# Latent attention scores from high and low parts: a two-block kernel on one core

## The chip, the cores and the metric

The kernel runs on one core of one Trainium2 chip. The core has the engines TensorE (PE), VectorE (DVE), ScalarE (ACT), GpSimd (POOL) and SyncE (SP, which issues most transfers), each with its own queue of instructions; semaphores order them. The metric is the device time of one execution in microseconds (us), median of several runs.

## The reference

Two blocks work on 512 tokens of 1024 features. The first block is untouched but for its last step, a norm, which is also the input norm of the second. What is computed in the second block (cut):

```python
h = _rms_norm(x, norm_g) * (1.0 + scale) + shift           # adaLN
dq, dk, dv, cq, ckv, kr, g = split(h @ w_in)
q_m = rms(cq) @ w_uq                                       # 4 heads x (128 nope + 64 rope)
k_nope = rms(ckv) @ w_uk ; v_m = rms(ckv) @ w_uv
q_m = _rms_norm(concat(q_nope, rope(q_pe)), mla_q_norm)
k_m = _rms_norm(concat(k_nope, rope(kr) for all heads), mla_k_norm)
logit_m = einsum('bqhd,bkhd->bhqk', q_m, k_m) * 192 ** -0.5        # latent heads
o_m = softmax(where(allowed, logit_m, -1e30)) @ v_m
logit_d = einsum('bqhcd,bkhcd->bchqk', dq, dk) * 64 ** -0.5 + bias  # 4 differential heads
attn_d = softmax(.)[:, 0] - lam * softmax(.)[:, 1]
o_d = _rms_norm(attn_d @ dv, diff_sub_norm) * (1 - lam_init)
out = x + gate * ((concat(o_d, o_m) * silu(g)) @ w_out)
```

## The kernel before

Data lie with features on the 128 rows and tokens along them (512 columns). Every projection is a product of three passes in the format fp32r: an operand is split into a high part (rounded) and a low part (the rest), and PE adds high by high, low by high and high by low (`mm3`, L962 to L964). The weights come in slabs; ACT copies the high part (`w_hi`, L582), DVE subtracts it for the low part (`weights_low`, L1610). Two slabs are in flight.

The final norm starts the second block: for each of eight feature tiles DVE computes hn (L1668), ACT copies h_hi (L650), POOL subtracts h_lo (L528), and PE opens its first projection tile. Behind the eight hn, DVE has the low part of the next weight slab, two step tiles of the bias and the reciprocal rsx, by which projections are scaled.

The projections that follow run in 34 numbered slots, one accumulation tile each; PE's `beside()` puts small matmuls between, and DVE's `evacuate()` empties the bank and does the slot's side work. Slots 26 to 33 are the eight tiles (128x256) of dv. In slots 28 to 33 the reciprocal norms of the latent heads are applied: PE's `widen` (L1034) spreads one row of `rs` over 128 rows of a bank, reading the 32 rows of `rs` of one quarter, and DVE's `scaled` (L1698) multiplies a tile of q (`qm`, tiles 0 to 3 nope, 4 and 5 the rope halves of two heads each), of k (`kn`) or of the rope part of k (`kp`) by it and by the gain. The list `WIDE` gives their order, two a slot.

The second attention consists of 32 units (`UNITS2`): v = 0 to 15 are latent, head v // 4 and query tile v % 4; v = 16 to 31 are differential. Each engine goes through them in a loop of its own:
- PE: `scores2(v + 2)`, `turn(v)` (four transposes of Pm, L1219), `values2(v - 1)` (L1516), and for v < 8 `widen_diff(v)` for dq and dk of the differential heads. A latent unit's scores are two fp32 matmuls: q nope by k nope (L1503) and the 64 rope rows (L1505).
- DVE: `weigh2(v)`, that is a reciprocal of the row sums (L1989) and the weighing of Pm (L2222; two operations, L2219 and L2220, in a differential unit), `peaks2(v + 2)` (mask or bias, and row maximum, L1974), for v < 8 `scaled` of dq or dk, and at v = 5, 9, 13 and so on `head_out`, a copy of a head's output out of its bank (L2226).
- ACT: `exps(v + 1)` (L747) and `evac(v)`, the copy of the turned Pm to PTm (L757). Scores of unit v + 2 wait for exp of unit v, whose bank they take.
- POOL adds the mask to the bias tiles of the differential heads (L533), which SP loads.

Then come the gate zg and the output projection.

## Time and profile before

| | us |
|---|---|
| median of three runs | 1823.74 (1819.90 to 1824.51) |
| the profiled execution | 1826.18 |
| its span | 1824.4 |
| PE busy | 1765.4 (97%) |
| DVE busy | 1030.8 (57%) |
| ACT busy | 627.8 (34%) |
| POOL busy | 86.0 (5%) |
| mean granted clock of PE | 0.990 |

An engine's busy time is the sum of its instructions in one profiled execution; the span runs from the first to the last. A chain of waits follows the end of the program back, from each piece of work to what released it. The granted clock is a share of 2.4 GHz. The final norm lies at 1441 to 1462 of the span, the second attention at 1604 to 1722.

### The profile page before, as it was taken

How to read it: one execution, taken by the hardware profiler on the slowest of the kernel's cores; microseconds unless marked ns; L12 is line 12 of the kernel's file. 1: busy time of each engine (PE TensorE's matmuls, PEld its weight loads, DVE VectorE, ACT ScalarE, POOL GpSimd, SP SyncE). 2: the span in 40 equal slices, each digit the busy share in tenths (PEclk: the TensorE clock that was granted, in tenths of full speed). 3: DMA queues.
4: the chain of work that ended last, by engine and by line, in shares of the span. 5: the costliest groups of instructions: out<-in, count | busy, mean ns of one | idle time of the engine just before them, and what ended most of it. 6: DMA issues, size and time to landing. Idle time of an engine off the chain costs nothing.

```text
span 1824.4 us, 22833 instructions
## 1 busy us (share of the span) xinstructions
PE 1765.4 (97%) x9171; PEld 1362.3 (75%) x9171; DVE 1030.8 (57%) x1645; ACT 627.8 (34%) x1047; POOL 86.0 (5%) x92
## 2 busy tenths in 40 slices
PE   7999999999988889999999999999999999999899
PEld 6888888887765557877888888888888666645677
DVE  5665444456566655437544457633544677756764
ACT  4221222231246761323322243312223566324631
POOL 0000000000012320000000000000000200011100
PEclk9999999899989999999999999999999999999999
DMA  6545332252200003212333233233332332201212
GB/s 215 182 165 187 113 108 76 64 186 94 70 1 1 2 1 115 82 58 70 93 101 106 93 99 92 86 94 110 94 100 80 89 101 94 86 23 36 73 59 89
DMA packets 232428, 163.60 MB, mean 90 GB/s; under 512 B 9372, under 2 KB 220548, under 8 KB 232196
## 3 DMA queue, kind: packets, MB, share of 16 engines
q1 hardware_dynamic: 230004, 157.95, 28.3%
q10 hardware_dynamic: 2320, 4.20, 0.6%
q8 instruction: 73, 1.20, 0.3%
q14 instruction: 31, 0.25, 0.0%
HBM read 155.84 MB, written 6.29 MB: 89 GB/s over the span
## 4 chain that ended last, share of the span: by engine, by line
PE 91%; DVE 6%; POOL 2%; issue 1%; SPq 0%; ACT 0%; DMA 0%; DVEq 0%
PE bank L962 24%; PE bank L964 24%; PE bank L963 24%; PE bank L1219 3%; PE bank L1207 2%; DVE bank L1974 2%; PE bank L1243 2%; PE bank L1386 1%; PE bank L1034 1%; PE bank L1041 1%; PE bank L1300 1%; PE bank L1516 1%; POOL Pm L521 1%; PE bank L1505 1%; PE bank L1174 1%
## 5 line engine op out<-in xcount | busy, mean ns | idle before, releaser
L962 PE MATMUL bank<-h_hi,w_hi 128*128 128x512 f32 x1200 | 478.9, 399 | 5.5 <-POOL h_lo L528 4.0
L964 PE MATMUL bank<-h_hi,w_lo 128*128 128x512 f32 x1200 | 467.5, 390 | 0.0
L963 PE MATMUL bank<-h_lo,w_hi 128*128 128x512 f32 x1200 | 467.5, 390 | 0.0
L582 ACT ACTIVATE w_hi<-w_raw 128x2048 fp32r<-128x2048 f32 (+3 forms) x134 | 236.8, 1767 | 525.2 <-PE bank L964 525.2
L1610 DVE TENSOR_TENSOR w_lo<-w_raw,w_hi 128x2048 fp32r<-128x2048 f32 (+3 forms) x134 | 283.4, 2115 | 56.9 <-ACT w_hi L582 54.5
L962 PEld LDWEIGHTS bank<-h_hi,w_hi 128*128 128x128 f32 x1200 | 225.3, 188 | 70.0 <-issue 17.7
L963 PEld LDWEIGHTS bank<-h_lo,w_hi 128*128 128x128 f32 x1200 | 225.3, 188 | 49.4 <-issue 4.1
L964 PEld LDWEIGHTS bank<-h_hi,w_lo 128*128 128x128 f32 x1200 | 225.2, 188 | 47.5
L962 PE MATMUL bank<-u_hi,w_hi 128*128 128x512 f32 x352 | 138.0, 392 | 0.0
L963 PE MATMUL bank<-u_lo,w_hi 128*128 128x512 f32 x352 | 137.9, 392 | 0.0
L964 PE MATMUL bank<-u_hi,w_lo 128*128 128x512 f32 x352 | 137.7, 391 | 0.0
L1616 DVE TENSOR_TENSOR act_f<-bank,rsx 128x512 f32<-128x512 f32 x44 | 30.4, 690 | 165.2 <-PE bank L964 165.2
L1219 PEld LDWEIGHTS bank<-cst,Pm 128*128 128x128 f32 x448 | 48.5, 143 | 89.3 <-POOL Pm L521 47.3
L747 ACT ACTIVATE Pm<-bank,mstat 128x512 f32<-128x512 f32 (+3 forms) x176 | 99.1, 572 | 34.8 <-DVE mstat L1974 33.3
L757 ACT ACTIVATE PTm<-bank 128x512 f32<-128x512 f32 (+3 forms) x160 | 68.1, 467 | 118.0 <-PE bank L1219 117.8
L1219 PE MATMUL bank<-cst,Pm 128*128 128x128 f32 x448 | 71.4, 289 | 33.3 <-POOL Pm L521 22.1
L697 ACT ACTIVATE silu<-silu 128x512 f32<-128x512 f32 x44 | 27.8, 632 | 199.2 <-DVE silu L1616 199.2
L1974 DVE CUSTOM_DVE_ANT_0 bank<-bank,mask 128x128 f32<-128x128 f32 (+3 forms) x128 | 60.5, 515 | 58.0 <-PE bank L1207 57.6
L521 POOL TENSOR_SCALAR Pm<-Pm,mstat,gates 128x128 f32<-128x128 f32 (+3 forms) x64 | 49.8, 779 | 628.6 <-DVE mstat L1989 628.6
L963 PEld LDWEIGHTS bank<-u_lo,w_hi 128*128 128x128 f32 x352 | 66.6, 189 | 14.0
L964 PEld LDWEIGHTS bank<-u_hi,w_lo 128*128 128x128 f32 x352 | 66.6, 189 | 13.9
L962 PEld LDWEIGHTS bank<-u_hi,w_hi 128*128 128x128 f32 x352 | 66.7, 189 | 13.9
(400 smaller groups left out, 2421.0 us busy)
## 6 DMA issues: line engine op xcount, KB each, us to landing
w_raw<-in_w_in SPq DMA_DIRECT2D x28, 1024.0 KB, 5.2
w_raw<-in_ffn_w_gate SPq DMA_DIRECT2D x44, 512.0 KB, 3.6
w_raw<-in_ffn_w_up SPq DMA_DIRECT2D x44, 512.0 KB, 4.8
w_raw<-in_ffn_w_down SPq DMA_DIRECT2D x32, 704.0 KB, 4.4
ada_w<-in_ada_w SPq DMA_DIRECT2D x16, 768.0 KB, 6.0
w_raw<-in_w_in SPq DMA_DIRECT2D x19, 512.0 KB, 4.0
w_raw<-in_w_out SPq DMA_DIRECT2D x8, 1024.0 KB, 5.0
w_raw<-in_w_branch_nsa SPq DMA_DIRECT2D x8, 512.0 KB, 5.1
```

Of the source, the lines that this page charges most:

```text
L521: pool.tensor_scalar(p_, p_, mstat[:, u % 2, 6:7], gates[:, t, g0:g0 + 1], ALU.mult, ALU.mult).then_inc(sem("p_ready"), 1)
L582: act.activation(w_hi[s % 2][:, 0:n], w_raw[s % 2][:, 0:n], ACT.Copy).then_inc(s_hi, 1)
L747: last = act.activation(Pm[u % 2][:, i, 0:n], bank[2 * (u % 2) + i][:, 0:n], ACT.Exp, bias=mstat[:, u % 2, 2 + i:3 + i], scale=scale, accu ...
L757: last = act.activation(PTm[u % 2][:, i, 0:n], bank[4 + i][:, 0:n], ACT.Copy)
L962: pe.matmul(o, l[0], r[0], start=first, stop=False)
L963: pe.matmul(o, l[0], r[1], start=False, stop=False)
L964: return pe.matmul(o, l[1], r[0], start=False, stop=last)
L1207: ins = pe.matmul(bank[2 * (u % 2) + e][:, 0:n], qT[r, hp, t * P:(t + 1) * P], kz[r, br, g, 0:n], start=True, stop=True)
L1219: ins = pe.transpose(bank[4 + i][:, b * P:(b + 1) * P], Pm[u % 2][:, i, b * P:(b + 1) * P], ident)
L1243: ins = pe.matmul(place(e, t), vtok[:, b, c:c + 64], PTm[u % 2][:, e, b * P:(b + 1) * P], start=u in FIRST and b == 0, stop=False)
L1610: dve.tensor_sub(w_lo[s % 2][:, 0:n], w_raw[s % 2][:, 0:n], w_hi[s % 2][:, 0:n]).then_inc(s_lo, 1)
L1974: return dve.tensor_tensor_reduce(s_, s_, add, -scale, 3.0e38, ALU.add, ALU.min, mstat[:, u % 2, 2 + i:3 + i])
```

## The change

1. Final norm: h_lo is subtracted by DVE (`low3`), one tile behind hn, instead of by POOL. The last square of the token norm is added by PE (a second matmul) and not by DVE.
2. dv tiles are evacuated by ACT with a scale for each row instead of by DVE.
3. `WIDE` has ten entries instead of twelve, in slots 28 to 32. The rope part of k is one tile for each head (`kp[h]`), both halves of its rows filled, a further DVE product by the bank that k uses.
4. `high_parts` on ACT copies four high parts for each head (q, k, rope of q on its own 64 rows, kp): heads 0 and 1 in slots 31 and 33, heads 2 and 3 behind `evac` of units 0 and 2. `low_part` on DVE subtracts the low parts: heads 0 and 1 in the same slots, heads 2 and 3 one part a unit, v = 0 to 7. The low half of rope q goes to the other 64 rows of `q_rope[h]`.
5. `weights_low` of the slab behind (zg's first) moves from slot 29 to slot 33.
6. A latent unit's scores are five fp32r matmuls: q_hi k_hi, q_hi k_lo, q_lo k_hi, and the stacked rope parts of 128 rows by kp_hi and by kp_lo.
7. Latent units are weighed by ACT (a Copy scaled by the reciprocal), between `exps(v + 1)` and `evac(v)`, instead of by DVE.
8. `widen_diff` and its `scaled` move from v = 0..7 to v = 8..15; the load of the first bias tiles waits for the scores of unit 7.

```diff
+        WH, WL = -32 + 8 * spare, -16 + 8 * spare
+        part = lambda name, kb, dt=F32R: at(name, [P, S], dt, ARENA + kb * KB)[:, :]
+        q_hi = [part(f"q_hi{h}", kb) for h, kb in enumerate((24, 40, WH, WL))]
+        k_hi = [part(f"k_hi{h}", kb) for h, kb in enumerate((26, 42, WH + 2, WL + 2))]
+        q_rope = [part(f"q_rope{h}", kb) for h, kb in enumerate((28, 44, WH + 4, WL + 4))]
+        kp_hi = [part(f"kp_hi{h}", kb) for h, kb in enumerate((30, 56, WH + 6, WL + 6))]
+        KP_AT = (48, 50, 58, 94)
+        kp = [part(f"kp{h}", kb, F32) for h, kb in enumerate(KP_AT)]
+        kp_lo = [part(f"kp_lo{h}", kb) for h, kb in enumerate(KP_AT)]
+        q_lo = at("q_lo", [P, 4, S], F32R, ARENA + 60 * KB)
+        k_lo = at("k_lo", [P, 4, S], F32R, ARENA + 72 * KB)
...
-                                sp.wait_ge(sem("wide_used"), 15)
+                                sp.wait_ge(sem("s_full"), U0 + 8)
...
-            for k in range(KD):
-                pool.wait_ge(sem("h_hi_ready"), 3 * KD + k + 1)
-                pool.tensor_sub(h_lo[:, k, :], hn[k % 4][:, :], h_hi[:, k, :]).then_inc(sem("h_ready"), 1)
...
-        WIDE = [("q", 0), ("k", 0), ("qp", 0), ("kp", 0), ("q", 1), ("k", 1), ("q", 2), ("k", 2), ("qp", 1), ("kp", 1), ("q", 3), ("k", 3)]
-        HEAD_WIDE = (7, 9, 13, 15)
+        WIDE = [("q", 0), ("k", 0), ("qp", 0), ("q", 1), ("k", 1), ("q", 2), ("k", 2), ("qp", 1), ("q", 3), ("k", 3)]
...
+            def high_parts(h):
+                e, done_wide = h % 2, (5, 8, 10, 13)[h]
+                own = slice(64 * e, 64 * e + 64)
+                act.wait_ge(sem("wide_used"), max(done_wide, 6 if h == 0 else 11 if h == 2 else 0))
+                act.activation(q_hi[h], qm[:, h, :], ACT.Copy).then_inc(sem("head_hi"), 1)
+                act.activation(k_hi[h], kn[:, h, :], ACT.Copy).then_inc(sem("head_hi"), 1)
+                act.activation(q_rope[h][own, :], qm[own, 4 + h // 2, :], ACT.Copy).then_inc(sem("head_hi"), 1)
+                act.activation(kp_hi[h], kp[h], ACT.Copy).then_inc(sem("head_hi"), 1)
...
+                act.wait_ge(acc_full, a + 1)
+                act.wait_ge(acc_free, a)
+                s, t = i // 4, i % 4
+                act.activation(dv[:, t, s * 256:(s + 1) * 256], bank[a % 4][:, 0:256], ACT.Copy, scale=col[:, G_RST + t:G_RST + t + 1]).then_inc(acc_free, 1)
+                if i == 4:
+                    for b in range(2):
+                        act.wait_ge(sem(f"bias_stored{b}"), 128)
+                if i in (5, 7):
+                    high_parts(i // 2 - 2)
...
             for v in range(len(UNITS2)):
...
+                if v < 16:
+                    act.wait_ge(sem("sum_ready"), attended(U0 + v))
+                    p0 = Pm[(U0 + v) % 2][:, 0, :]
+                    act.activation(p0, p0, ACT.Copy, scale=mstat[:, (U0 + v) % 2, 6:7]).then_inc(sem("pm_ready"), 1)
                 evac(U0 + v, S, 1)
+                if v in (0, 2):
+                    act.wait_ge(acc_full, first_acc["zg"])
+                    high_parts(2 + v // 2)
...
                 if n == 3:
-                    pe.wait_ge(sem("sqg_added"), 7)
-                    pe.matmul(bank[4][:, :], ones, sqgsum[:, :], start=True, stop=True).then_inc(sem("gmm"), 1)
+                    pe.wait_ge(sem("sqg_added"), 6)
+                    pe.matmul(bank[4][:, :], ones, sqgsum[:, :], start=True, stop=False)
+                    pe.wait_ge(sem("nsqg"), KD)
...
+                if U0 <= u < U0 + 16:
+                    pe.wait_ge(sem("pm_ready"), u - U0 + 1)
+                else:
+                    pe.wait_ge(sem("p_ready"), attended(u) if u < U0 else attended(u) - 16)
...
-                if 28 <= slot < 34:
+                if 28 <= slot < 33:
                     for what, i in WIDE[2 * slot - 56:2 * slot - 54]:
-                        if what in ("q", "k"):
+                        if what == "qp":
+                            widen(2, i, 4, 2)
+                        else:
                             widen(2, (0, 2)[what == "k"] + i // 2, 4 + i % 2)
-                        else:
...
-                if t == 0:
-                    pe.wait_ge(sem("wide_used"), HEAD_WIDE[h] if kind else 17 + 2 * h)
+                if t == 0 and kind:
+                    pe.wait_ge(sem("head_split"), 4 * h + 4)
+                elif t == 0:
+                    pe.wait_ge(sem("wide_used"), 15 + 2 * h)
...
-                    pe.matmul(bank[b][:, :], qm[:, h, q], kn[:, h, :], start=True, stop=False)
-                    r = slice(64 * (h % 2), 64 * (h % 2) + 64)
-                    ins = pe.matmul(bank[b][:, :], qm[r, 4 + h // 2, q], kp[r, h // 2, :], start=False, stop=True)
+                    pe.matmul(bank[b][:, :], q_hi[h][:, q], k_hi[h], start=True, stop=False)
+                    pe.matmul(bank[b][:, :], q_hi[h][:, q], k_lo[:, h, :], start=False, stop=False)
+                    pe.matmul(bank[b][:, :], q_lo[:, h, q], k_hi[h], start=False, stop=False)
+                    pe.matmul(bank[b][:, :], q_rope[h][:, q], kp_hi[h], start=False, stop=False)
+                    ins = pe.matmul(bank[b][:, :], q_rope[h][:, q], kp_lo[h], start=False, stop=True)
...
-                if v < 8:
-                    widen_diff(v)
+                if 8 <= v < 16:
+                    widen_diff(v - 8)
...
-                if n == 3:
+                if n == 3 and k < KD - 1:
...
+                def low3(k):
+                    dve.wait_ge(sem("h_hi_ready"), 3 * KD + k + 1)
+                    tick(dve.tensor_sub(h_lo[:, k, :], hn[k % 4][:, :], h_hi[:, k, :]), "h_ready")
                 dve.wait_ge(sem("token_std"), 1)
                 for k in range(KD):
                     if k >= 4:
                         dve.wait_ge(sem("h_ready"), 3 * KD + k - 3)
                     dve.wait_ge(sem("xg_ready"), k + 1)
                     tick(dve.scalar_tensor_tensor(hn[k % 4][:, :], std[:, :], col[:, G_MOD + k:G_MOD + k + 1], xg[:, k, :], ALU.mult, ALU.add), "hn_ready")
+                    if k:
+                        low3(k - 1)
+                low3(KD - 1)
...
+            def spread(what, i):
+                if what == "k":
+                    j = count.get("wide_used", 0)
+                    dve.wait_ge(sem("wide_full"), j + 1)
+                    done(dve.scalar_tensor_tensor(kp[i], ckr[:, 1, :], col[:, G_KP:G_KP + 1], wide_bank(j)[:, :], ALU.mult, ALU.mult))
+                    scaled(kn[:, i, :], kn[:, i, :], G_KN)
+                elif what == "q":
+                    scaled(qm[:, i, :], qm[:, i, :], G_QN)
+                else:
+                    scaled(qm[:, 4 + i, :], qm[:, 4 + i, :], G_QP)
+            def low_part(h, i):
+                own, other = (slice(64 * e, 64 * e + 64) for e in (h % 2, 1 - h % 2))
+                dve.wait_ge(sem("head_hi"), 4 * h + i + 1)
+                if i == 0:
+                    ins = dve.tensor_sub(q_lo[:, h, :], qm[:, h, :], q_hi[h])
+                elif i == 1:
+                    ins = dve.tensor_sub(k_lo[:, h, :], kn[:, h, :], k_hi[h])
+                elif i == 2:
+                    ins = dve.tensor_sub(q_rope[h][other, :], qm[own, 4 + h // 2, :], q_rope[h][own, :])
+                else:
+                    ins = dve.tensor_sub(kp_lo[h], kp[h], kp_hi[h])
+                tick(ins, "head_split")
...
-                    scale_rows(dst, t, 256)
+                    acc_at[0] += 1
...
-                if slot >= 28:
-                    for j in (2 * slot - 56, 2 * slot - 55):
-                        scaled(*spread[j])
+                if 28 <= slot < 33:
+                    for what, i in WIDE[2 * slot - 56:2 * slot - 54]:
+                        spread(what, i)
+                if slot in (31, 33):
+                    for i in range(4):
+                        low_part((slot - 31) // 2, i)
...
-                if slot in (1, 3, 5, 7, 9, 15, 17, 25, 29):
+                if slot in (1, 3, 5, 7, 9, 15, 17, 25, 33):
...
+                if kind:
+                    return
...
-                else:
-                    tick(dve.tensor_scalar(p0, p0, st[:, 6:7], None, ALU.mult), "p_ready")
...
                 if v < 8:
-                    d = (dq, dk)[v % 2][:, v // 2, :]
+                    low_part(2 + v // 4, v % 4)
+                elif v < 16:
+                    d = (dq, dk)[v % 2][:, v // 2 - 4, :]
                     scaled(d, d, (G_DQ, G_DK)[v % 2])
                 if v >= 5 and v % 4 == 1:
```

DVE from the end of the dv slots to the first reciprocal of the attention (L1974 and L2024 are the peaks; each has a second row that reads its result). Before:

```order
L1619 TENSOR_SCALAR dv<-bank,col 128x256
L1698 SCALAR_TENSOR_TENSOR qm<-qm,col,bank 128x512
L1698 SCALAR_TENSOR_TENSOR kn<-kn,col,bank 128x512
L1974 ISA bank,mstat<-bank,cst 128x512
L1974 ISA mstat 128x1
L1974 ISA bank,mstat<-bank,hidden_215 128x512
```

After:

```order
L1748 SCALAR_TENSOR_TENSOR kn<-kn,col,bank 128x512
L2194 TENSOR_TENSOR q_lo<-qm,q_hi_227 128x512
L2196 TENSOR_TENSOR k_lo<-kn,k_hi_231 128x512
L2198 TENSOR_TENSOR q_rope_235<-qm,q_rope_235 64x512
L2200 TENSOR_TENSOR kp_lo_247<-kp_243,kp_hi_239 128x512
L1654 TENSOR_TENSOR w_lo_60<-w_raw_56,w_hi_58 128x2048
L2024 ISA bank,mstat<-bank,cst 128x512
L2024 ISA mstat 128x1
L2024 ISA bank,mstat<-bank,hidden_214 128x512
```

Four low parts of head 1 and the low part of zg's first slab now stand ahead of the first peaks; the evacuation of dv (L1619) is gone.

DVE in the loop of the attention, at v = 4 and 5 before and v = 8 and 9 after, where the second of the two has a `head_out` (L2226, now L2302). Before:

```order
L1698 SCALAR_TENSOR_TENSOR dq<-dq,col,bank 128x512
L1989 RECIPROCAL mstat<-mstat 128x1
L2222 TENSOR_SCALAR Pm_123<-Pm_123,mstat 128x512
L1974 ISA bank,mstat<-bank,cst 128x512
L1974 ISA mstat 128x1
L1698 SCALAR_TENSOR_TENSOR dk<-dk,col,bank 128x512
L2226 COPY cst<-bank 128x512
L1989 RECIPROCAL mstat<-mstat 128x1
L2222 TENSOR_SCALAR Pm_122<-Pm_122,mstat 128x512
```

After:

```order
L1748 SCALAR_TENSOR_TENSOR dq<-dq,col,bank 128x512
L2039 RECIPROCAL mstat<-mstat 128x1
L2024 ISA bank,mstat<-bank,cst 128x512
L2024 ISA mstat 128x1
L1748 SCALAR_TENSOR_TENSOR dk<-dk,col,bank 128x512
L2302 COPY cst<-bank 128x512
L2039 RECIPROCAL mstat<-mstat 128x1
L2024 ISA bank,mstat<-bank,cst 128x512
L2024 ISA mstat 128x1
```

The weighing (L2222) no longer follows the reciprocal; the scaled products (now L1748) stand ahead of the reciprocal as before, in the later units.

ACT from the first exp on (L747, now L755; L757, now L765). Before:

```order
L747 ACT_TABLE_LOAD
L747 ACTIVATE Pm_122,mstat<-bank,mstat 128x512
L747 ACTIVATE Pm_123,mstat<-bank,mstat 128x512
L757 ACTIVATE PTm_124<-bank 128x512
L747 ACTIVATE Pm_122,mstat<-bank,mstat 128x512
L757 ACTIVATE PTm_125<-bank 128x512
```

After:

```order
L755 ACTIVATE Pm_122,mstat<-bank,mstat 128x512
L755 ACTIVATE Pm_123,mstat<-bank,mstat 128x512
L952 ACTIVATE Pm_122<-Pm_122,mstat 128x512
L765 ACTIVATE PTm_124<-bank 128x512
L919 ACTIVATE q_hi_228<-qm 128x512
L920 ACTIVATE k_hi_232<-kn 128x512
L921 ACTIVATE q_rope_236<-qm 64x512
L922 ACTIVATE kp_hi_240<-kp_244 128x512
L755 ACTIVATE Pm_122,mstat<-bank,mstat 128x512
L952 ACTIVATE Pm_123<-Pm_123,mstat 128x512
```

The weighing (L952) stands between exp and the copy of the turned unit, and the four Copies of head 2 (L919 to L922) stand behind the copy of unit 0 and ahead of exp of unit 2.

## Rows read from the trace of the kernel before

**Rows 1.** windows; columns: stretch, us, busy PE PEld DVE ACT POOL, clock, DMA

```profile
1612.00:1648.00 36.00, 35.76 (x157) 16.96 (x158) 18.94 (x43) 9.91 (x25) 1.77 (x2) 1.00 0.00 0
1648.00:1667.00 19.00, 19.00 (x94) 10.54 (x93) 8.45 (x25) 7.09 (x18) 0.00 (x0) 1.00 0.00 1
```

**Rows 2.** timeline of the final norm: start, length, engine, work, idle before

```profile
1446.07 1.41 DVE L1668 SCALAR_TENSOR_TENSOR tmp<-std,col,xg 128x512 f32<-128x512 f32 x2 [1.79 <-ACT std L643]
...
1451.44 1.79 DVE L1668 SCALAR_TENSOR_TENSOR tmp<-std,col,xg 128x512 f32<-128x512 f32 x1
...
1461.12 0.50 PE L962 MATMUL bank<-h_hi,w_hi 128*128 128x512 f32 x1 [1.62 <-POOL h_lo L528]
```

**Rows 3.** chain of waits: start, length, what; final norm, then one matmul

```profile
1447.56 13.51 POOL h_lo L528 x7
...
1461.62 0.23 PE bank L963
```

**Rows 4.** ScalarE (ACT) and VectorE work by form, whole span: count, busy, mean ns

```profile
L614 ACT ACTIVATE h_hi<-x,col 128x512 fp32r<-128x512 f32 x20 | 14.3, 713 | 36.8 <-DVE x L2117 24.1 <-DVE x L1613 7.6 <-DVE x L1852 5.1
...
L650 ACT ACTIVATE h_hi<-tmp 128x512 fp32r<-128x512 f32 x4 | 2.5, 626 | 0.9 <-DVE tmp L1668 0.9
...
L1610 DVE TENSOR_TENSOR w_lo<-w_raw,w_hi 128x2048 fp32r<-128x2048 f32 x98 | 225.6, 2303 | 44.3 <-ACT w_hi L582 42.4
...
L1637 DVE TENSOR_TENSOR sqsum<-sqsum,sq 128x512 f32<-128x512 f32 x12 | 8.3, 688 | 0.2
```

**Rows 5.** chain of waits, slots before the second attention

```profile
1562.08 1.84 PE bank L1018 x8
...
1598.91 1.02 PE bank L1034 x8
```

**Rows 6.** timeline, first turn of the second attention

```profile
1610.30 0.66 PE L1219 MATMUL bank<-cst,Pm 128*128 128x128 f32 x4
```

**Rows 7.** chain of waits, a latent unit with a widening

```profile
1643.47 1.00 PE bank L1034 x4
1644.47 1.06 PE bank L1503 x2
1645.53 1.05 PE bank L1505 x2
...
1647.16 0.89 PE bank L1516 x8
```

**Rows 8.** chain of waits, a unit with head_out

```profile
1635.08 0.76 DVE dk L1698
...
1635.86 0.70 DVE cst L2226
...
1636.58 0.17 DVE mstat L1989
```

**Rows 9.** chain of waits around the end of the second attention

```profile
1715.58 0.56 DVE Pm L2219
...
1716.16 0.76 DVE Pm L2220
```

**Rows 10.** windows of granted clock, after idle PE; columns as in rows 1

```profile
494.00:499.00 5.00, 1.00 (x6) 0.50 (x6) 4.58 (x19) 1.92 (x9) 0.51 (x1) 1.00 0.00 0
499.00:506.00 7.00, 5.84 (x22) 2.61 (x20) 5.25 (x23) 2.71 (x12) 1.42 (x3) 0.50 0.02 5
506.00:512.50 6.50, 6.50 (x29) 4.58 (x30) 1.46 (x7) 2.10 (x8) 0.48 (x1) 0.50 0.00 0
...
1716.00:1717.00 1.00, 0.03 (x1) 0.03 (x1) 0.96 (x3) 0.28 (x2) 0.00 (x0) 1.00 0.00 0
...
1718.00:1721.00 3.00, 3.00 (x17) 3.00 (x16) 0.36 (x1) 0.86 (x2) 0.00 (x0) 0.51 0.00 0
1721.00:1724.00 3.00, 3.00 (x21) 2.69 (x20) 0.69 (x1) 0.85 (x2) 0.00 (x0) 1.00 0.02 5
```

**Rows 11.** timeline, PE's first wait for the final norm

```profile
1449.41 0.47 PE L962 MATMUL bank<-h_hi,w_hi 128*128 128x512 f32 x1 [2.42 <-POOL h_lo L528]
```

More of the change, by code:

```diff
@@ L406, in build @@
         N_VEC_DMAS = len(VECS) - 1 + 2 * len(HALF_VECS)
+        pair_units = lambda hp, ts: [(hp, t, br) for t in ts for br in range(2)]
+        second = pair_units(1, (3, 2, 1, 0))
+        UNITS = pair_units(0, range(NT))
+        for t in range(NT):
+            UNITS += [(None, t, None), second[t]]
+        COMPRESSED = len(UNITS) - 2
+        UNITS += second[4:]
+        for hp in range(2, 8):
+            UNITS += pair_units(hp, range(NT))
+        U0 = len(UNITS)
+        FIRST = [min(u for u in range(U0) if UNITS[u][0] == hp) for hp in range(8)]
+        FULL_AT = {COMPRESSED: 0}
+        for hp in range(1, 8):
+            FULL_AT[max(u for u in range(U0) if UNITS[u][0] == hp)] = hp
+        attended = lambda u: u + 1 - sum(1 for w in UNITS[:u + 1] if w[0] is None)
         @block.sync
@@ L493, in _ @@
             sp.wait_ge(sem("out_stored"), 32 * NT)
-        pair_units = lambda hp, ts: [(hp, t, br) for t in ts for br in range(2)]
-        second = pair_units(1, (3, 2, 1, 0))
-        UNITS = pair_units(0, range(NT))
-        for t in range(NT):
-            UNITS += [(None, t, None), second[t]]
-        COMPRESSED = len(UNITS) - 2
-        UNITS += second[4:]
-        for hp in range(2, 8):
-            UNITS += pair_units(hp, range(NT))
-        U0 = len(UNITS)
-        FIRST = [min(u for u in range(U0) if UNITS[u][0] == hp) for hp in range(8)]
-        FULL_AT = {COMPRESSED: 0}
-        for hp in range(1, 8):
-            FULL_AT[max(u for u in range(U0) if UNITS[u][0] == hp)] = hp
-        attended = lambda u: u + 1 - sum(1 for w in UNITS[:u + 1] if w[0] is None)
         @block.gpsimd
@@ L915, in _ @@
             each_slab("ukv", rest_squares, 8)
-            each_slab("dv", all_norms, 4)
+            each_slab("dv", diff_values, 4)
             exps(U0, 0, S, 1, -1.0)
@@ L1005, in big_norm @@
                 if n == 3:
-                    pe.wait_ge(sem("sqg_added"), 7)
-                    pe.matmul(bank[4][:, :], ones, sqgsum[:, :], start=True, stop=True).then_inc(sem("gmm"), 1)
+                    pe.wait_ge(sem("sqg_added"), 6)
+                    pe.matmul(bank[4][:, :], ones, sqgsum[:, :], start=True, stop=False)
+                    pe.wait_ge(sem("nsqg"), KD)
+                    pe.matmul(bank[4][:, :], ones, sqg[(KD - 1) % 2][:, :], start=False, stop=True).then_inc(sem("gmm"), 1)
                 pe.wait_ge(sem("sq_added"), 7 * n)
@@ L1440, in beside @@
                     pe.wait_ge(sem("bias_out"), 16)
-                if 28 <= slot < 34:
+                if 28 <= slot < 33:
                     for what, i in WIDE[2 * slot - 56:2 * slot - 54]:
-                        if what in ("q", "k"):
+                        if what == "qp":
+                            widen(2, i, 4, 2)
+                        else:
                             widen(2, (0, 2)[what == "k"] + i // 2, 4 + i % 2)
-                        else:
-                            widen(2, (0, 2)[what == "kp"] + i, 4, 2)
             def widen_diff(j):
@@ L2127, in _ @@
             STEPS_BEHIND = {1: 2, 2: 1, 3: 2, 4: 1, 5: 2, 6: 2, 7: 1, 8: 2, 16: 2}
-            spread = [(qm[:, i, :], qm[:, i, :], G_QN) if what == "q" else (kn[:, i, :], kn[:, i, :], G_KN) if what == "k"
-                      else (qm[:, 4 + i, :], qm[:, 4 + i, :], G_QP) if what == "qp" else (kp[:, i, :], ckr[:, 1, :], G_KP) for what, i in WIDE]
+            def spread(what, i):
[20 more added lines that the diff above has]
+                tick(ins, "head_split")
             def evacuate(dst, t=None):
@@ L2142, in evacuate @@
                     copy_tile(dst)
-                freed()
+                if t is None:
+                    freed()
                 if slot == 3:
@@ L2161, in evacuate @@
                     dve.wait_ge(sem("rst_full"), 2)
-                    done(dve.tensor_copy(col[:, G_RST:G_RST + NT], bank[4][:, 0:NT]))
+                    done(dve.tensor_copy(col[:, G_RST:G_RST + NT], bank[4][:, 0:NT]), "rst_ready")
                 if slot == 26:
```

12 lines of the change are left out of this document (6 added, 6 removed).

## Prediction

> **What bounds the kernel now.** Read the table of the profile first: TensorE (PE) is busy for 97% of the span, so an edit pays only where PE waits or where PE's own work gets shorter. Then the windows of the second attention: from 1612 to 1648, where each unit also carries a widening, PE is busy 35.76 of 36.00 us, and from 1648 to 1667, latent units alone, 19.00 of 19.00, while VectorE (DVE) is busy for about half of either and ScalarE (ACT) for under 0.4 [rows 1]. PE is the bound there. The chain of waits gives one such unit piece by piece: widening 1.00, scores 1.06 and 1.05, transposes 0.59, values 0.89, in all 4.59 [rows 7]. Outside the attention, the place to see is the final norm: the chain passes through GpSimd (POOL) for 13.51 us, PE starts only after 2.42 idle and stands idle 1.62 before the last of the eight tiles [rows 2, 3, 11].
>
> **Final norm: −2.0.** The eight h_lo subtractions leave POOL, where seven take 13.51 [rows 3], for DVE. DVE's own steps there cost 0.70 each when POOL is silent (1.41 for two) and up to 1.79 beside it [rows 2]; a 128x512 subtraction or sum of two SBUF tiles is 0.69 [rows 4]. Sixteen at 0.70 from 1446.07, with 0.4 for the first wait on ACT, end at 1457.7, where POOL ended at 1461.07. Next on DVE is the low part of the following weights, 2.30 [rows 4], so it is ready at about 1460.2 and PE opens its second projection tile there. Before, that tile began six matmuls of 0.23 [rows 3] after 1461.12, at 1462.5. That is −2.3; I take −2.0 for the hops between engines. Bounds: the idle of 1.62 goes at least, less 0.4 of hops (−1.2); at most DVE keeps nothing of its queue in PE's way and the 3.4 less 0.3 come through (−3.1). That PE adds the last square itself (one fp32 matmul more) I take at nothing: ACT's table load stands behind that spot and covers it; uncovered, about 0.5.
>
> **The dv slots: +0.9.** The pairs of widenings stand in five slots instead of six, −1.0 (1.02 for eight matmuls, one pair [rows 5]). But the pair (q-rope 0, q 1) now reads the same 32 rows of rs twice. The nearest rows: eight small matmuls of alternating row groups take 1.02, and eight where groups repeat take 1.84 [rows 5]; so +0.8. PE then waits for ACT, which now evacuates dv behind its Copies, which take 0.63 each [rows 4]: a wait of about half a Copy in each of three slots and one hop, +1.1. Bounds 0 (no wait, the pair overlaps) to +1.9. The four extra DVE products for the rope part of k (0.75 each) lie in slots where PE works for 4 us and DVE for about 2: nothing, and as much as 0.75 for the last of them.
>
> **Start of the attention: +2.0.** Before, the last dv matmul is followed 7.4 us later by the first turn, at 1610.30 [rows 6]. After (in before's time), from 1602.9: dv evacuation 0.4, then ACT's four high parts of head 1, each 0.63 long [rows 4] and about 0.52 apart, and DVE's four low parts of 0.69 behind them, until 1606.9; then w_lo of zg's first slab, 2.30, which now stands straight ahead of the first peaks (the first piece of order), until 1609.2; peaks 0.7, exp 0.69, peaks of unit 1, exp, and ACT's weighing 0.71 [rows 4], so that the first turn is at 1612.3. Bounds: +0.5 (w_lo alone, partly under the scores) and +3.5 (Copies at their full length and no overlap).
>
> **Units 0 to 7: −9.1.** Before, from the turn at 1610.30 to the end of the scores at 1646.58: 36.2 for eight units [rows 6, 7]. After, the widening is gone and the latent scores are five single-pass matmuls of 0.23 [rows 3] with 0.1 for the switch of type: 1.25 instead of 2.11. PE's unit is 0.66 + 0.89 + 1.25 = 2.8. Six units at 2.85 are 17.1. In units 0 and 2, ACT has four Copies more, behind its evacuation and ahead of the next exp (the third piece of order): 0.5 + 4 x 0.52 + 0.69 + 0.71 + turn 0.66 = 4.65, twice 9.3. With 0.4 for head_out at unit 5 and 0.3 of hops, 27.1. Bounds: 22.8 (ACT hidden) and 31 (weighing on ACT holds every unit up by 0.5).
>
> **Units 8 to 15: +9.6.** The widenings land here, and with cheap scores there is nothing left to hide DVE's answer. DVE's order is peaks, scaled dq or dk, head_out, reciprocal (the second piece of order); the reciprocal of the next unit stands behind scaled, which waits for the widening, which PE runs after turn and values. So each step is turn 0.66, values 0.89, widening 1.00, scaled 0.76, reciprocal 0.17 [rows 6 to 8], ACT's weighing 0.71 [rows 4], with hops 4.33. Seven steps are 30.3, and head_out [rows 8] at units 9 and 13 adds 1.4: 31.7. Before, they took 22.0, all of it PE's work [rows 1]: five steps of 3.39 (4.59 less the widening and the 0.2 by which the scores' first matmul is longer behind one) and two of 2.54, whose scores are those of a differential unit (1.06). The last step, to unit 16, waits in the same way and has the two DVE operations of a differential unit, 0.56 and 0.76 [rows 9]: +0.9, at most +1.9. What the change gains in the first half is given back in the second: the total of the widenings is the same, the saved scores (16 x 0.86 = 13.8) turn into waits for DVE and ACT.
>
> Sum so far: −2.0 + 0.9 + 2.0 − 9.1 + 9.6 + 0.9 = +2.3. The later stages are the same; POOL's bias sums, which stood in units 0 to 3, stand at units 7 to 9 and finish long before unit 16 asks for them.
>
> **The clock: +2.1.** In my walk PE has no work between the scores of unit 1 (about 1605.8) and those of unit 2 (about 1610.6), which wait for exp: over 4.5 us idle, just before the attention. What rows show: with PE busy 1.00 of 5 us its granted clock was 0.50 for the 13.5 us from 499 to 512.5; after some 2 us idle (0.03 busy from 1716 to 1717) it was 0.51 for 3 us and back at 1.00 from 1721 [rows 10]; after 2.42 idle at 1449.41 it stayed at 1.00 [rows 11]. So a fall to 1.2 GHz is likely. At half clock a unit of 2.8 takes 5.6; a dip like the shorter one (some 4.2 us) costs half its length, 2.1.
>
> The Trainium skill ("TensorE: Matmul & The Clock Gate", section "Why this matters for your kernels") speaks against the change here: an idle gap between bursts of matmuls sends the clock back to half. By that rule the sum is +4.4, and by the row at 1449.41, where a gap was forgiven, it is +2.3.
>
> Total +4.4. The profiled execution of before took 1826.18 (span 1824.4), so after's would be 1830.6; the median of before is 1823.74, and the forecast for the median is 1828.1, no change within 0.3% (5.5 us, about what a measurement of this kernel can tell).
>
> **Rivals.**
> - *The clock holds* (0.18): +2.3, 1826.0. For it stands the row at 1449.41; against it the length of this gap.
> - *Slower: the low clock lasts as long as at 499* (0.22). Price: for 13.5 us at 1.2 GHz, PE-bound units of 5.6 against 3.6 on average, so 2.4 units done where 3.7 would be: 4.8 us lost. 2.3 + 4.8 = +7.1, 1830.8. It decides against the forecast once the dip lasts over about 6 us. For it: units 0 and 2 leave PE idle for 2 of their 4.65 us, as thin a load as from 499 to 506.
> - *Slower: ACT is the bound of the first half too* (0.10): exp, weighing, evacuation and the wait between them hold each unit up by 0.5; 8 x 0.5 = 4 more on top of the forecast, +8.4, 1832.1. Rows for it: none of before has ACT between the reciprocal and the turn; against it, ACT's busy time of 1.9 in a unit of 2.8.
> - *Faster: the second half is bound by PE* (0.10). If the reciprocal came before scaled, a unit would be 0.66 + 0.89 + 1.00 + 1.15 = 3.7: 8 x 0.63 + 1.4 = 6.4 less, with the final norm at its better end 1.1 less: 2.3 − 7.5 = −5.2, and −6.0 if the row groups overlap as well: 1817.7. The clock must hold too. The order of DVE speaks against it.
> - *It doesn't do what it says*: the five passes are not 0.23 apart, since each switches between tiles of another row count. 0.2 more for each unit in the PE-bound half, +1.6: +6.0, 1829.7 (0.06). For it, the first scores matmul is 1.06 behind a widening of 32 rows [rows 7], longer than elsewhere; against it, every fp32r triple stands 0.23 apart.
>
> **How the numbers follow.** The forecast has a chance of 0.34. Faster by over 0.3%: 0.10. Slower: 0.22 + 0.10 + 0.06 = 0.38. Within: 0.34 + 0.18 = 0.52. The range goes from the faster rival, 1817.5, to 1835: the rival with ACT (+8.4) and the upper ends of the norm (0.8), the dv slots (1.0) and the last step (1.0), +11.2.
>
> **What would show it.** In the profile after: the last h_lo near 1457.7 and no POOL work from 1440 to 1470; an idle PE of over 4 us just before the first turn and a clock of 0.5 behind it; units 0 to 7 about 27 us long, with two of 4.6; units 8 to 15 at 4.3 with PE waiting for ACT's Pm, and 5.0 at the two with head_out. It would be wrong if units 8 to 15 run at 3.7, if the first units are as slow as the last, or if the clock never falls.

## The result

| | before | changed |
|---|---|---|
| median, 11 runs each | 1822.79 us (1817.98 to 1825.25) | 1829.15 us (1825.87 to 1834.14) |
| ratio to before | | 1.0036, 95% interval 1.0025 to 1.0047 |
| span of the profiled execution | 1824.4 us | 1826.9 us |
| mean granted clock | 0.990 | 0.988 |

The change costs 6.6 us (4.6 to 8.6), by the ratio. The forecast was 1828.1, +4.4; the time lies in its range. The forecast gave a slowing of over 0.3% a chance of 0.38 and a time within 0.3% one of 0.52; 0.36% is just on the slow side of that line, and the interval holds both sides. Of all executions of the kernels in this document one, of the kernel with latent units weighed by DVE, took 9859.93 us; its ratio leaves it out, and nothing here explains it.

The windows of the changed kernel, by the same columns as [rows 1]:

```profile
1440.00:1480.00 40.00, 38.48 (x230) 24.64 (x232) 35.05 (x45) 26.88 (x39) 0.00 (x0) 1.00 0.26 85
...
1604.00:1612.00 8.00, 5.36 (x20) 4.25 (x19) 2.89 (x8) 4.77 (x12) 0.00 (x0) 0.71 0.00 0
1612.00:1648.00 36.00, 31.70 (x178) 23.89 (x177) 16.16 (x38) 20.89 (x44) 5.90 (x4) 0.93 0.09 30
1648.00:1667.00 19.00, 15.44 (x85) 8.61 (x84) 8.64 (x22) 9.32 (x19) 1.26 (x1) 1.00 0.04 14
```

PE, which had 35.76 of 36 us and 19.00 of 19 in before [rows 1], has 31.70 and 15.44: PE no longer bounds these units by itself, and its clock falls in them. ACT's busy time in the first of the two stretches has doubled (20.89 for 9.91).

**By stage.** From the start of one piece of work to the start of the next, in the timelines of both traces, from the final norm's table load (1443.87 before, 1439.08 after; the 4.8 us ahead of it are told below):

| stretch | before | changed | difference | forecast |
|---|---|---|---|---|
| table load to the first step matmuls | 23.00 | 18.49 | −4.5 | −2.0 |
| to the first scores of the attention | 137.10 | 138.91 | +1.8 | +2.9 |
| first scores to turn 0 | 6.33 | 9.20 | +2.9 | (in the line above) |
| turn 0 to turn 8 | 36.21 | 29.29 | −6.9 | −9.1 |
| turn 8 to turn 15 | 22.04 | 31.94 | +9.9 | +9.6 |
| turn 15 to turn 16 | 4.14 | 5.84 | +1.7 | +0.9 |
| turn 16 to turn 31 | 46.43 | 49.27 | +2.8 | 0 |
| turn 31 to the end | 105.28 | 104.88 | −0.4 | 0 |
| the clock, by itself | | | (within the lines) | +2.1 |

The second block takes 7.3 us longer. The spans differ by 2.5 only, for in this pair of executions the changed kernel came to the table load 4.8 us earlier, in code that is the same.

### The profile page after: what moved, and what is told of

It is laid out like the page before. It is cut to its first block, busy times and chain, and to the rows that moved or that the text cites. A ratio compares the mean times of both kernels' runs of the same rounds, so it can differ in the third digit from the quotient of the medians.

```text
span 1826.9 us, 22889 instructions
## 1 busy us (share of the span) xinstructions
PE 1756.9 (96%) x9181; PEld 1370.0 (75%) x9181; DVE 1027.3 (56%) x1646; ACT 650.2 (36%) x1087; POOL 71.1 (4%) x84
## 4 chain that ended last, share of the span: by engine, by line
PE 90%; DVE 6%; issue 1%; ACT 1%; POOL 1%; SPq 0%; DMA 0%; DVEq 0%; ACTq 0%
PE bank L997 25%; PE bank L998 24%; PE bank L999 24%; PE bank L1259 3%; PE bank L1244 2%; PE bank L1283 2%; DVE bank L2024 2%; PE bank L1071 1%; PE bank L1426 1%; PE bank L1078 1%; PE bank L1340 1%; PE bank L1560 1%; POOL Pm L533 1%; PE bank L1211 1%; DVE Pm L2297 1%
## 5 line engine op out<-in xcount | busy, mean ns | idle before, releaser
L755 ACT ACTIVATE Pm<-bank,mstat 128x512 f32<-128x512 f32 (+3 forms) x176 | 99.0, 572 | 17.7 <-DVE mstat L2024 16.4
L765 ACT ACTIVATE PTm<-bank 128x512 f32<-128x512 f32 (+3 forms) x160 | 68.1, 467 | 99.7 <-PE bank L1259 99.5
L2024 DVE CUSTOM_DVE_ANT_0 bank<-bank,mask 128x128 f32<-128x128 f32 (+3 forms) x128 | 60.5, 514 | 56.9 <-PE bank L1244 56.5
L1902 DVE SCALAR_TENSOR_TENSOR x<-bank,x 128x512 f32<-128x512 f32 x32 | 22.1, 691 | 95.2 <-PE bank L999 95.2
```

The lines of the kernel that those rows point to most:

```text
L755: last = act.activation(Pm[u % 2][:, i, 0:n], bank[2 * (u % 2) + i][:, 0:n], ACT.Exp, bias=mstat[:, u % 2, 2 + i:3 + i], scale=scale, accu ...
L765: last = act.activation(PTm[u % 2][:, i, 0:n], bank[4 + i][:, 0:n], ACT.Copy)
L2024: return dve.tensor_tensor_reduce(s_, s_, add, -scale, 3.0e38, ALU.add, ALU.min, mstat[:, u % 2, 2 + i:3 + i])
```

## What the traces show

**Final norm.** Timeline of before (the last two of POOL's eight subtractions), then of the changed kernel:

```profile
1457.75 4.74 POOL L528 TENSOR_TENSOR h_lo<-sqg,h_hi 128x512 fp32r<-128x512 f32 x2
```

```profile
1443.56 0.47 PE L997 MATMUL bank<-h_hi,w_hi 128*128 128x512 f32 x1 [1.52 <-DVE h_lo L1709]
...
1452.28 2.29 DVE L1654 TENSOR_TENSOR w_lo<-w_raw,w_hi 128x2048 fp32r<-128x2048 f32 x1
...
1454.67 0.45 PE L997 MATMUL bank<-h_hi,w_hi 128*128 128x512 f32 x1
```

POOL's last pair ends at 1462.49. The 13.51 of [rows 3] are seven of eight subtractions, and 1461.07 is the end of the seventh; the forecast took it for the end of all. In the changed kernel DVE keeps ahead of PE, which needs 1.37 for the six matmuls of each h_lo and shows no wait after its start at 1443.56. The low part of the weights ends at 1454.57 and PE opens the next tile at 1454.67, when the 48 matmuls ahead of it are done: it holds nothing up.

**Start of the attention and its clock.** Timeline and windows of the changed kernel:

```profile
1603.52 0.65 PE L1545 MATMUL bank<-k_hi,q_hi 128*128 128x512 f32 x1 [4.48 <-ACT Pm L755]
...
1610.78 1.12 PE L1259 MATMUL bank<-cst,Pm 128*128 128x128 f32 x4 [2.64 <-ACT Pm L952]
```

```profile
1599.10:1603.50 4.40, 0.00 (x0) 0.00 (x0) 4.21 (x6) 1.79 (x4) 0.00 (x0) 1.00 0.00 0
1603.80:1607.10 3.30, 3.30 (x11) 2.61 (x11) 0.76 (x2) 1.27 (x4) 0.00 (x0) 0.50 0.00 0
1608.20:1610.80 2.60, 0.03 (x1) 0.03 (x1) 1.85 (x6) 2.52 (x6) 0.00 (x0) 0.95 0.00 0
1610.80:1613.60 2.80, 2.80 (x13) 2.80 (x14) 0.00 (x0) 1.67 (x4) 0.00 (x0) 0.50 0.00 0
1617.50:1619.70 2.20, 0.00 (x0) 0.00 (x0) 1.47 (x4) 2.15 (x5) 0.00 (x0) 1.00 0.00 0
1620.80:1624.10 3.30, 3.30 (x13) 2.71 (x12) 0.30 (x1) 1.50 (x4) 0.00 (x0) 0.50 0.02 5
1670.60:1672.70 2.10, 0.00 (x0) 0.00 (x0) 2.06 (x3) 0.00 (x0) 1.03 (x1) 0.83 0.00 0
1672.70:1678.40 5.70, 5.65 (x20) 3.92 (x21) 3.28 (x10) 1.94 (x5) 1.27 (x1) 0.50 0.15 46
```

Four idle stretches of PE (0.00 to 0.03 busy, the first number behind the length), and each is followed by matmuls at half clock: 4.4 us idle before the scores of unit 2, about 2.6 and 2.2 in units 0 and 2 while ACT makes the high parts of heads 2 and 3, and 2.1 before turn 16. The forecast had one dip, of 4.2 us. There are four, three of about 3 us and one of about 6. A fifth, from 1719.6 to 1723.2, has its like in before, behind 1717 [rows 10].

**Units 8 to 15.** The chain of waits of the changed kernel, a unit without head_out and the head of one with it:

```profile
1636.51 1.03 PE bank L1071 x4
...
1637.57 0.76 DVE dq L1748
...
1638.35 0.18 DVE mstat L2039
...
1638.55 0.73 ACT Pm L952
...
1639.32 0.66 PE bank L1259 x4
1639.98 0.89 PE bank L1560 x8
...
1641.92 0.76 DVE dk L1748
...
1642.71 0.70 DVE cst L2302
```

It is the forecast's chain link for link (widening, scaled, reciprocal, weighing, turn, values): 4.36 us from turn to turn, and 5.08 where head_out stands in it. [Rows 7] had PE's own work in this place.

## The experiments

All medians and ratios are of several runs beside the kernel before on the same chip; the changed kernel stands at 1.0036.

### The final norm by itself

The kernel before, with DVE's subtractions alone (the last square stays with DVE):

```diff
             for k in range(KD):
-                pool.wait_ge(sem("h_hi_ready"), 3 * KD + k + 1)
-                pool.tensor_sub(h_lo[:, k, :], hn[k % 4][:, :], h_hi[:, k, :]).then_inc(sem("h_ready"), 1)
...
+                    if k:
+                        low3(k - 1)
+                low3(KD - 1)
```

> The kernel before with one part of the change: the eight h_lo subtractions of the final norm by DVE, alternating with hn; all else as before. Theory from the two traces: PE reached the first step matmuls of the second projection tile 23.07 us after the norm's table load in before and 18.56 after it in after, so this part alone gives about -4.5 us (ratio 0.9975). Rival, the forecast's own term: -2.0 (0.9989), with the low part of the weights (2.3) ahead of PE's second tile. Second rival: nothing, since the eight subtractions only move the wait to the evacuation.

1816.35 us, ratio 0.9974 (0.9959 to 0.9988): −4.7 us. The first step matmuls come 18.50 behind the table load, in the changed kernel 18.49: the square that PE adds costs nothing, for from the step matmuls ahead of it to the table load both take 2.71. So the rest of the change costs 1.0036 − 0.9974, about 11 us.

### The reciprocal ahead of the scaled product

```diff
+            early = lambda v: 9 <= v < 17
             for v in range(len(UNITS2)):
-                weigh2(v)
+                if not early(v):
+                    weigh2(v)
                 if v + 2 < len(UNITS2):
                     peaks2(v + 2)
+                if early(v + 1):
+                    weigh2(v + 1)
```

> The changed kernel with one difference: for units 9 to 16 DVE does the reciprocal of the row sums (and unit 16's two weighing operations) ahead of the scaled dq or dk of the unit before, not behind it. Theory: in units 8 to 15 the chain widening, scaled, reciprocal, ACT's weighing, turn is what ends last (4.36 us a unit, 5.08 with head_out); taken out of it, PE's own work of 3.7 to 3.8 us a unit remains, and the stretch from turn 8 to turn 16 (37.8 us) falls to about 30.5 to 31.5: -6 to -7 us against the changed kernel, about level with before (ratio 1.000). Rival: ACT's queue (exp, weighing, copy) is the bound there, and the stretch falls by under 2.

1820.40 us, 0.9986 (0.9972 to 0.9999): −9 us against the changed kernel. Its chain of waits in this stretch is PE alone:

```profile
1642.13 1.00 PE bank L1071 x4
1643.14 0.43 PE bank L1545
1643.56 0.23 PE bank L1546
1643.79 0.24 PE bank L1547
1644.03 0.23 PE bank L1548
1644.26 0.24 PE bank L1549
1644.50 0.44 PE bank L1259 x4
1644.94 0.89 PE bank L1560 x8
```

That is 3.69 a unit. Turn 8 to 15 took 26.13 for 31.94, turn 15 to 16 3.54 for 5.84: −8.1, more than the 6 to 7 expected. With the idle stretch ahead of turn 16 the dip behind it went too (3.11 from turn 16 to 17 for 4.77). ACT's queue is not the bound here. This was the forecast's rival on the fast side, which it set aside because the order of DVE speaks against it: rightly for the kernel as it was, and the cure is that order.

### PE kept busy where it was idle

```diff
             scores2(1)
+            for _ in range(5):
+                pe.matmul(bank[1][:, :], ident[:, :], hidden[3], start=True, stop=True)
...
+                if v in (1, 3):
+                    for _ in range(2):
+                        pe.matmul(bank[1][:, :], ident[:, :], hidden[3], start=True, stop=True)
                 turn(U0 + v, NT, 1)
```

> The changed kernel with fp32 matmuls of 128x512 that nothing reads added on PE, where it is idle: five ahead of the scores of unit 2 (4.48 us idle), two ahead of the turns of units 1 and 3 (2.64 and 2.26 idle). Theory: idle PE is what takes the clock to half; kept busy it stays at 1.00, the three dips near 1604, 1611 and 1621 (3.2 us each) go, and the stretch from the first scores of unit 2 to turn 4 is 2 to 3.5 us shorter: -2 to -3.5 against the changed kernel. Rival: the dips are not tied to the idle stretches, the clock falls as often, and the time is the same or up to 1 us more for fillers that stick out.

1824.48 us, 1.0009 (0.9995 to 1.0024): −4.9 us with added work that nobody needs. Windows of this kernel over the first units:

```profile
1606.00:1612.00 6.00, 5.82 (x21) 3.05 (x20) 4.33 (x8) 2.64 (x7) 0.00 (x0) 1.00 0.00 0
1612.00:1620.00 8.00, 6.84 (x39) 4.88 (x38) 3.73 (x10) 6.51 (x15) 0.00 (x0) 1.00 0.00 0
1620.00:1630.00 10.00, 9.46 (x55) 7.02 (x55) 4.29 (x12) 7.71 (x17) 0.00 (x0) 1.00 0.05 6
```

All at 1.00. First scores to turn 0 took 8.32 (9.20 in the changed kernel), turn 0 to 8 26.21 (29.29): 4.0 us of the two stretches were the three dips. That is nearly half of what PE had stood idle in these places (9.4), on top of it. Later in the attention, where nothing was filled, the same trace shows two idle stretches:

```profile
1663.00:1664.70 1.70, 0.23 (x2) 0.00 (x1) 1.66 (x5) 0.72 (x1) 0.00 (x0) 1.00 0.00 0
1664.70:1668.20 3.50, 3.50 (x14) 2.67 (x16) 0.55 (x2) 1.93 (x5) 0.34 (x1) 0.53 0.20 75
1674.30:1676.50 2.20, 0.00 (x0) 0.00 (x0) 2.17 (x3) 0.00 (x0) 1.46 (x1) 1.00 0.00 0
1676.50:1680.00 3.50, 3.38 (x23) 2.43 (x24) 3.31 (x10) 2.12 (x6) 0.00 (x0) 1.00 0.28 75
```

Behind the shorter one, 1.47 ahead of turn 15, the clock fell (+1.6, a dip that the changed kernel doesn't have), and behind the longer one, 2.2 ahead of turn 16, it held: turn 16 to 17 took 2.70, where the changed kernel with the same wait took 4.77. So filling the idle stretches removed the dips behind them, but an idle stretch does not by its length decide whether a dip follows. The Trainium skill ("TensorE: Matmul & The Clock Gate", section "Why this matters for your kernels") warns of idle gaps between bursts; this run agrees with it, as the dips behind the three that were filled are gone. It warns of longer gaps than the 2.64 and 2.26 that had a dip behind them here; there the measurement decides.

### The weights' low part back in slot 29

```diff
-                if slot in (1, 3, 5, 7, 9, 15, 17, 25, 33):
+                if slot in (1, 3, 5, 7, 9, 15, 17, 25, 29):
```

> The changed kernel with the low part of zg's first weight slab (DVE, 2.3 us) back in slot 29, as before the change, instead of ahead of the first peaks. Theory: it stands on the path to the first exp, so the first turn comes 2.2 us earlier, PE's idle stretch shrinks from 4.5 to 2.3 us, and the clock may hold there: -2.2 to -3.5 against the changed kernel. Rival: slot 29 has no room on DVE and the 2.3 reappear as a PE wait for the widening banks in slots 30 and 31: no gain.

1827.19 us, 1.0018 (1.0004 to 1.0033): about −3.3, in an interval that overlaps that of the changed kernel; the trace shows where it comes from. First scores to turn 0: 6.12 for 9.20, that is 2.2 of DVE work and 0.9 of a dip that is gone. Turn 0 to 8 took 27.65 for 29.29, with one dip less. The slots took the same time (138.87 from the step matmuls to the first scores, 138.91 in the changed kernel), so slot 29 had room.

### Widenings of like width paired

```diff
-        WIDE = [("q", 0), ("k", 0), ("qp", 0), ("q", 1), ("k", 1), ("q", 2), ("k", 2), ("qp", 1), ("q", 3), ("k", 3)]
+        WIDE = [("q", 0), ("k", 0), ("qp", 0), ("qp", 1), ("q", 1), ("k", 1), ("q", 2), ("k", 2), ("q", 3), ("k", 3)]
...
-                e, done_wide = h % 2, (5, 8, 10, 13)[h]
+                e, done_wide = h % 2, (5, 9, 11, 13)[h]
```

> The changed kernel with another order of the ten widenings: both rope halves of q (two matmuls of 64 columns each) stand as one pair, instead of one beside q of head 1 and one beside k of head 2. Theory: in the changed kernel both mixed pairs take 2.05 us on PE where pairs of like width take 1.02 to 1.06, although the second mixed pair reads two different groups of 32 rows; what runs one after the other is the different width of the output, so all five pairs at about 1.05 give -2.0 against the changed kernel. Rival, the forecast's reason (the same 32 rows read twice, in the first mixed pair alone): -1.0.

1827.64 us, 1.0028 (1.0015 to 1.0041): −1.5, an interval that by itself leaves the size open; the chain of waits does not. A mixed pair of the changed kernel:

```profile
1586.69 2.05 PE bank L1071 x6
```

and two rows of this one, pairs of two halves each and of two whole widths:

```profile
1583.77 1.02 PE bank L1071 x8
1587.84 1.06 PE bank L1071 x4
```

From the step matmuls to the first scores it took 136.86 for 138.91, −2.05. The mixed pair shown is k of head 2 (rows 96 to 127 of rs) and q-rope of heads 2 and 3 (rows 32 to 63): different rows, and still one after the other. The forecast's reason, the same 32 rows read twice, would have spared this pair. That the width of the output is what matters fits all rows seen here; whether it is the columns or the change of form between two matmuls was not separated.

### High parts one a unit

```diff
-                if v in (0, 2):
+                if v < 8:
                     act.wait_ge(acc_full, first_acc["zg"])
-                    high_parts(2 + v // 2)
+                    high_parts(2 + v // 4, (v % 4,))
```

The low parts of heads 2 and 3 follow one unit later, v = 1 to 8.

> The changed kernel with the eight high parts of heads 2 and 3 on ACT one a unit (units 0 to 7) instead of four behind unit 0 and four behind unit 2, and the low parts one unit later. Theory: units 0 and 2 (5.10 and 4.91 us, PE idle 2.64 and 2.26 in them) fall to about 3, and two of the three clock dips go with the idle stretches: turn 0 to turn 8 from 29.3 to 24 to 25.5, -4 to -5 against the changed kernel. Rival: one Copy of 0.5 a unit on ACT makes all eight units ACT-bound at 3.4 and the stretch is 27 or more.

1826.82 us, 1.0014 (1.0001 to 1.0026): −4. Turn 0 to 8 took 25.79 for 29.29, but not as the theory had it in full: six of the eight units take 3.14 where PE needs 2.5. The long units are gone and one dip of the three is left. Later a dip ahead of turn 15 is new (+1.6) and the one behind turn 16 is missing (−2.1), as with the fillers. Each unit has the chain of turn, ACT's copy of it, one high part, exp and weighing, as the rival said, at a lower price than it said.

### Latent units weighed by DVE

```diff
-                if v < 16:
-                    act.wait_ge(sem("sum_ready"), attended(U0 + v))
-                    p0 = Pm[(U0 + v) % 2][:, 0, :]
-                    act.activation(p0, p0, ACT.Copy, scale=mstat[:, (U0 + v) % 2, 6:7]).then_inc(sem("pm_ready"), 1)
...
+                else:
+                    tick(dve.tensor_scalar(p0, p0, st[:, 6:7], None, ALU.mult), "p_ready")
```

> The changed kernel with latent units weighed by DVE again, behind the reciprocal. Theory: ACT's weighing is a link of 0.73 plus hops in the chain of units 8 to 15 where DVE's is 0.50: 4.1 instead of 4.36 a unit, and 0.7 less ACT work in units 0 to 7: -2 to -3 against the changed kernel. Rival: DVE's longer queue delays the peaks of the next units by 0.5 each and the gain is nothing.

1822.45 us, 0.9992 (0.9980 to 1.0004): −8 us, far more than the 2 to 3 expected. Turn 8 to 15 is 30.32 for 31.94, 4.12 a unit, as expected. The surprise is turn 0 to 8: 23.63 for 29.29. In unit 0, turn 1 no longer stands behind four high parts on ACT:

```profile
1611.49 0.16 DVE L2032 RECIPROCAL mstat<-mstat 128x1 f32<-128x1 f32 x1
1611.68 0.49 DVE L2291 TENSOR_SCALAR Pm<-Pm,mstat 128x512 f32<-128x512 f32 x1
1611.78 0.62 ACT L922 ACTIVATE kp_hi<-kp 128x512 fp32r<-128x512 f32 x1
...
1612.22 0.66 PE L1252 MATMUL bank<-cst,Pm 128*128 128x128 f32 x4 [1.16 <-DVE Pm L2291]
```

DVE weighs unit 1 while ACT still copies, and PE waits 1.16 instead of 2.64; two of the three dips are not there. The other units take 2.5 to 3.4.

### The widenings back in units 0 to 7

```diff
-                if 8 <= v < 16:
-                    widen_diff(v - 8)
+                if v < 8:
+                    widen_diff(v)
```

and the scaled products with them, behind the low parts.

> The changed kernel with the eight widenings of dq and dk and their products back in units 0 to 7. Theory: the chain widening, scaled, reciprocal, weighing costs its 4.36 us wherever it stands, but in units 0 to 7 it also covers ACT's high parts, which cost PE there on their own in the changed kernel: turn 0 to 8 about 36, turn 8 to 16 about 23 to 24, together 60 against 67 in the changed kernel: -6 to -8 with the dips that go. Rival: low part and scaled both stand ahead of the reciprocal and add up to 5 us a unit, 40 + 23.5, and the time is -3 at best.

1821.61 us, 0.9988 (0.9975 to 1.0001): −9. Turn 0 to 8 took 38.55: 5.10 and 4.97 in units 0 and 2, 5.97 in unit 1 with a dip, 5.09 with head_out, and 4.36 in the other four. Turn 8 to 16 22.32 (19.45 and 2.87): 60.9 for 67.1. The theory holds (the chain costs 4.36 wherever it stands), and the rival, 5 us a unit, falls. So 6 of the 9 us are the place of the widenings; most of the rest is turn 16 to 31 (45.60 for 49.27), without the dip behind turn 16. The eight units with them cost about the same in either place (38.55 and 37.78), the eight without them 22.3 here and 29.3 in the changed kernel, where they carry the high parts: under the chain of a widening a part of those is hidden, and in the cheap units nothing is.

### All of it together

The changed kernel with DVE's weighing, the reciprocal and weighing of units 1 to 16 early, the high parts one a unit, the low part in slot 29 and the paired widths. No new lines beside those of the diffs above, except `early = lambda v: 1 <= v < 17`.

> The changed kernel with what the single experiments gave, together: latent units weighed by DVE; the reciprocal and the weighing of units 1 to 16 ahead of the low part or scaled product of the unit before; high parts of heads 2 and 3 one a unit; the weights' low part in slot 29; like widths paired in the widenings. Theory: with every chain out of PE's way the attention is bound by PE, 2.5 to 2.7 us a unit without and 3.6 to 3.7 with a widening: turn 0 to 8 about 21, turn 8 to 16 about 29.5, the first turn 2 to 3 us earlier: about -17 against the changed kernel and -10 to -12 against before (ratio 0.994). Rival: the parts overlap (each single gain was partly the same clock dips and the same wait), and the sum is level with the kernel before with the norm alone, 0.9974.

1807.11 us, 0.9905 (0.9889 to 0.9920), four executions on another chip than the kernels above, beside before there: −17 us against before and −24 against the changed kernel; faster than theory. Turn 0 to 8 took 20.89, turn 8 to 16 29.08. PE's wait ahead of the scores of unit 2 and two of the scores matmuls a little later:

```profile
1605.90 0.50 PE L1537 MATMUL bank<-k_hi,q_hi 128*128 128x512 f32 x1 [2.28 <-ACT Pm L755]
...
1608.38 0.63 PE L1538 MATMUL bank<-k_lo,q_hi 128*128 128x512 f32 x1
```

The starts behind the second are 0.43 apart and not 0.23: one dip is left at the start of the attention (a second lies behind turn 17). The next kernel puts two matmuls into the idle stretch:

```diff
             scores2(1)
+            for _ in range(2):
+                pe.matmul(bank[1][:, :], ident[:, :], hidden[3], start=True, stop=True)
```

> The same kernel with two fp32 matmuls that nothing reads on PE ahead of the scores of unit 2. Theory: the idle stretch left there is about 2.3 us, of which they take 1.7, so a dip of the clock at the start of the attention goes if there is one: -1 against the one without. Rival: the stretch is too short for a dip, and the fillers change nothing.

1806.06 us, 0.9902 (0.9886 to 0.9917), five executions. Turn 0 to 8 took 19.40, −1.5: the dip is gone in the trace. The two medians don't tell the kernels apart.

## Why the prediction was right, and where it was not

- **Final norm**, −2.0 forecast, −4.5 measured. The step that failed is the reading of [rows 3]: the eighth h_lo ends 1.4 after the seventh, so in the kernel before the first tile ended at 1464.0 and not at 1462.5. Of the other 1.0, 0.7 is that PE opened the next tile 15.59 behind the table load (1454.67) and not 16.3: DVE's sixteen operations took 11.1 and not 11.6, and PE, which started 0.9 sooner (1.52 idle for 2.42 [rows 11]), was done by then too. The last 0.3 had been taken off for hops. The upper bound of −3.1 fell with the same misreading.
- **dv slots and start**, +0.9 and +2.0 forecast, +4.7 measured, of which 0.9 is clock. Two mixed pairs cost a full 1.0 more each, not one of them 0.8; the row of 1.84 that the 0.8 came from [rows 5] is of matmuls that read all 128 rows and write 32, no widenings. The wait for ACT's dv evacuation was 0.56, not 1.1. The walk of the start was right link for link: low parts until 1599.8, w_lo, peaks, exp; the idle stretch of 4.48 stood as "over 4.5".
- **Units 0 to 7**, −9.1 without the clock, −6.9 with it. 3.1 of the 29.29 went with the fillers, which leaves 26.2, 0.9 under the forecast's 27.1. The mechanism was right. The forecast had the two units bound by ACT, and its rival with the long clock even counts 2 us of idle PE in each, but it priced no dip behind them.
- **Units 8 to 15**, +9.6 forecast (its terms give +9.7), +9.9 measured, and the experiment with the early reciprocal shows that it is the named wait.
- **Turn 16**, +0.9 forecast with +1.9 as the other end, +1.7 measured, and 2.1 more behind it (4.77 from turn 16 to 17, 2.71 before): a dip of 6 us follows its idle stretch, where none follows before's shorter wait. That the wait brought it is not shown: in the kernel with the fillers the same wait has none behind it. The turn in before and in the changed kernel:

```profile
1672.69 0.66 PE L1219 MATMUL bank<-cst,Pm 128*128 128x128 f32 x4 [1.53 <-DVE Pm L2220]
```

```profile
1672.75 1.12 PE L1259 MATMUL bank<-cst,Pm 128*128 128x128 f32 x4 [2.23 <-DVE Pm L2298]
```

- **The clock**, +2.1 forecast. The fillers give 4.0 for the start and the first units, and the dip at turn 16 costs about 2.1 (4.77 from turn 16 to 17 for 2.71): about 6 in this execution. It was the term with the largest error, put at a third of what it was. What failed is the count of dips: one at the start, where four came. The rival "the low clock lasts as long as at 499" had nearly the size (+4.8) by another mechanism: no long stretch, but four shorter ones. Its argument that units 0 and 2 are as thin a load as from 499 to 506 misreads [rows 10], where PE was busy 5.84 of 7 us.

So the forecast lay 2 us under the measured change, since its two large errors, −2.5 in the norm and +4.0 in the clock, cancel for the most part; that the total came so close is luck. The reading that the change trades a bound on PE for waits on DVE and ACT was right. It didn't ask the next question, what the waits would be worth if they were arranged otherwise: nearly all of them were the order of instructions, not work.

## What to carry to other kernels

When an edit makes the bounding engine's share of a loop cheaper, write down the chain of the others per turn of the loop before and after: here 3.7 us of PE against 4.36 of a chain that nobody had to wait in, and one reciprocal moved up in the queue was worth 9 us. The waits of over 2 us on PE were paid twice here, once as a wait and once in clock, so it was worth splitting a block of four operations in another engine's queue, and even matmuls without a purpose paid. And count the pieces of a row (x7 of 8) before its end is taken for the end of the work.
